# How the softmax sums of two attentions reach the rows of their heads: eight products, or one product and a broadcast by DMA

## The reference

```
# sparse attention (dsa): the keys outside a query's top 128 are masked
logits = (q . k) * scale - slope[head] * |q_pos - k_pos|    # masked where not selected
p = softmax(logits);  out = p @ v
# latent attention (mla): q and k of 64 + 32 features from latent projections
logits = (q . k) * scale                                    # masked after the query's chunk of 64
p = softmax(logits);  out = p @ v
```

## Time and profile before

| | |
|---|---|
| median of 3 runs | 2496.99 us (2496.9 to 2497.02) |
| the profiled execution: time, span | 2499.49 us, 2497.7 us |
| mean granted TensorE clock | 0.997 |
| busy: TensorE, weight load, VectorE, ScalarE, GpSimd | 99%, 79%, 54%, 40%, 44% |
| sparse attention, latent attention | about 1456 to 1502 us, 2025 to 2071 us |

### The profile page before, as it was taken

The page is one execution under the profiler, slowest core; times in us unless marked ns, Lnnn a source line. Parts: engine busy times, 40 slices in busy tenths (PEclk is TensorE's granted clock), DMA queues, the critical chain, the costliest instruction groups (busy, mean ns, idle before and its releaser), DMA issues.

```text
span 2497.7 us, 31897 instructions
## 1 busy us (share of the span) xinstructions
PE 2460.7 (99%) x11826; PEld 1975.9 (79%) x11826; DVE 1351.0 (54%) x2136; ACT 988.2 (40%) x1386; POOL 1102.8 (44%) x560
## 2 busy tenths in 40 slices
PE   9999999999999999999999999999999999999998
PEld 6658888887777788888877878888888758888887
DVE  7856635634666465365338655551554465652553
ACT  6553222235555432223334254532344243532333
POOL 7844444444332344444443413544444313544443
PEclk9999999999999999999999999999999999999999
DMA  7535546533322365564353312324333122324322
GB/s 205 151 91 171 186 142 202 164 89 110 98 68 72 88 208 165 164 195 135 90 146 85 102 34 77 94 76 117 93 87 91 64 68 68 85 80 114 100 76 70
DMA packets 403610, 282.09 MB, mean 113 GB/s; under 512 B 10867, under 2 KB 382707, under 8 KB 403484
## 3 DMA queue, kind: packets, MB, share of 16 engines
q1 hardware_dynamic: 389660, 230.09, 32.6%
q10 hardware_dynamic: 13824, 50.34, 5.4%
HBM read 269.73 MB, written 2.12 MB: 109 GB/s over the span
## 4 chain that ended last, share of the span: by engine, by line
PE 92%; DVE 3%; ACT 3%; issue 1%; POOL 1%; DMA 0%; SPq 0%; DVEq 0%; ACTq 0%
PE ps L762 27%; PE ps L763 27%; PE ps L764 27%; PE ps L1387 1%; PE ps L1583 1%; PE ps L1149 1%; PE ps L1123 1%; PE ps L1262 1%; PE ps L1237 1%; PE ps L1111 1%; PE ps L1108 1%; DVE u_lo L1746 1%; PE ps L1525 0%; ACT weight_hi L2728 0%; PE ps L1251 0%
## 5 line engine op out<-in xcount | busy, mean ns | idle before, releaser
L2582 POOL TENSOR_TENSOR weight_lo<-weight_raw,weight_hi 128x1024 fp32r<-128x1024 f32 (+3 forms) x416 | 940.4, 2282 | 1316.2 <-ACT weight_hi L2728 1193.5
L764 PE MATMUL ps<-u_hi,weight_lo 128*128 128x512 f32 (+1 forms) x2424 | 916.1, 378 | 0.0
L762 PE MATMUL ps<-u_hi,weight_hi 128*128 128x512 f32 (+1 forms) x2216 | 866.1, 391 | 8.1 <-POOL weight_lo L2582 2.0
L763 PE MATMUL ps<-u_lo,weight_hi 128*128 128x512 f32 (+1 forms) x2216 | 855.8, 386 | 0.0
L2728 ACT ACTIVATE weight_hi<-weight_raw 128x2048 fp32r<-128x2048 f32 (+2 forms) x213 | 363.2, 1705 | 576.0 <-PE ps L764 544.1
L764 PEld LDWEIGHTS ps<-u_hi,weight_lo 128*128 128x128 f32 x2424 | 455.8, 188 | 85.6
L762 PEld LDWEIGHTS ps<-u_hi,weight_hi 128*128 128x128 f32 x2216 | 416.1, 188 | 114.2 <-issue 15.8
L763 PEld LDWEIGHTS ps<-u_lo,weight_hi 128*128 128x128 f32 x2216 | 416.3, 188 | 84.7 <-issue 2.9
L764 PE MATMUL ps<-act_hi,weight_lo 128*128 128x512 f32 (+1 forms) x748 | 281.5, 376 | 0.0
L762 PE MATMUL ps<-act_hi,weight_hi 128*128 128x512 f32 (+1 forms) x704 | 269.5, 383 | 0.0
L763 PE MATMUL ps<-act_lo,weight_hi 128*128 128x512 f32 (+1 forms) x704 | 269.2, 382 | 0.0
(11 more groups left out here) (347 smaller groups left out, 2753.2 us busy)
## 6 DMA issues: line engine op xcount, KB each, us to landing
weight_raw<-in_ffn_w_up SPq DMA_DIRECT2D x132, 512.0 KB, 5.2
arena<-in_ada_w ACTq DMA_DIRECT2D x96, 512.0 KB, 5.7
weight_raw<-in_ffn_w_down SPq DMA_DIRECT2D x64, 704.0 KB, 4.7
weight_raw<-in_ffn_w_gate SPq DMA_DIRECT2D x44, 512.0 KB, 4.0
weight_raw<-in_ev_w_in SPq DMA_DIRECT2D x10, 1024.0 KB, 6.2
weight_raw<-in_conv_w_pw SPq DMA_DIRECT2D x16, 512.0 KB, 6.3
weight_raw<-in_ple_w_gate SPq DMA_DIRECT2D x16, 512.0 KB, 3.8
weight_raw<-in_attn_w_qkv SPq DMA_DIRECT2D x16, 512.0 KB, 5.4
```

The source lines that it names most:

```text
L762: pe.matmul(bank, w[0], x[0], start=start, stop=False)
L763: pe.matmul(bank, w[0], x[1], start=False, stop=False)
L764: return pe.matmul(bank, w[1], x[0], start=False, stop=stop)
L2582: low_part = pool.tensor_tensor(w_lo[r][:, cols], raw[r][:, cols], w_hi(k0 + j)[:, cols].bitcast(F32), ALU.subtract)
```

## The change

In the spreads with a = 0, 2 and 4 of both attentions, TensorE makes one product instead of eight: `rowinv`, 8 columns wide, is the stationary operand and the identity the moving one, so that 8 rows of 128 come out (head, then block). ScalarE copies the 8 rows to SBUF (`inverse_rows`), waits for that copy, and stores them to a table in device memory (`inverse_kept`) on its own queue. In the next odd step, after its three first exponentials, it waits for the store and issues a second transfer that reads each head's 4 rows as one row of 512 and repeats it on the head's 64 partitions of `sq[0]`. VectorE's multiply waits for that transfer instead of ScalarE's copy. The last spread of each attention (a = 6) stays as it was.

```diff
+        inverse_kept = nc.dram_tensor("inverse_kept", [6, 2 * NB, P], F32).ap()
...
+        inverse_rows = tmp[0:2 * NB, S:S + P]
...
+        spread_stored, spread_landed = sem("spread_stored"), sem("spread_landed")
...
                     if a > 0:
                         pe.wait_ge(spread_copied, p0 + a // 2)
+                    if a < G - 2:
+                        pe.matmul(ps[0:2 * NB, 3, 0:P], rowinv[:, 0:2 * NB], ident, start=True, stop=True).then_inc(sums_spread, 1)
+                        return
                     for b in range(NB):
...
-                        dve.wait_ge(spread_copied, n.next(spread_copied))
+                        copied = n.next(spread_copied)
+                        if g < G + 1:
+                            dve.wait_ge(spread_landed, n.next(spread_landed, 16))
+                        else:
+                            dve.wait_ge(spread_copied, copied)
                         dve.tensor_tensor(act_tmp[(g - 3) // 2 % 2], ps[:, 2], sq[0], ALU.mult).then_inc(o_copied, 1)
...
                         for b in range(NB - 1):
                             exponential(g, b)
+                        if g % 2 == 1 and g >= 3:
+                            kept = inverse_kept[3 * (kind == "mla") + g // 2 - 1]
+                            sc.wait_ge(spread_stored, n.next(spread_stored, 16))
+                            sc.dma_start(sq[0], bass.AP(kept.tensor, kept.offset, [[S, 2], [0, 64], [1, S]])).then_inc(spread_landed, 16)
...
                         if g >= 4:
                             sc.wait_ge(o_copied, o1 + g // 2 - 1)
-                        sc.activation(sq[0], ps[:, 3], ACT.Copy).then_inc(spread_copied, 1)
+                        if g < G:
+                            kept = inverse_kept[3 * (kind == "mla") + g // 2 - 1]
+                            sc.activation(inverse_rows, ps[0:2 * NB, 3, 0:P], ACT.Copy).then_inc(spread_copied, 1)
+                            sc.wait_ge(spread_copied, n.next(spread_copied))
+                            sc.dma_start(kept, inverse_rows).then_inc(spread_stored, 16)
+                        else:
+                            sc.activation(sq[0], ps[:, 3], ACT.Copy).then_inc(spread_copied, 1)
+                            n.take(spread_copied, 1)
```

## The result

The changed kernel takes 2510.14 us (median of 6 runs, 2508.0 to 2511.63) against 2496.94 for the kernel before (6 runs, 2496.55 to 2498.75): 13.2 us or 0.5% slower, ratio 1.0051, interval 1.0041 to 1.0062. The forecast was slower, 2519 in a range of 2506 to 2546.

A forecast was written before the change was run, and what follows sets the result against it. TensorE, busy 99% of the span, was taken to bound the kernel before; late broadcasts would cost 19.0 us with TensorE's gain inside, plus 3 for the clock: +22 us on 2496.99, so 2519.0, range 2506 to 2546.

The forecast's parts named there:

- What bounds the pairs: VectorE's multiply in odd steps would wait 3 to 5 us in six places for a broadcast shared by 2 engines.
- L: Time from the broadcast's issue to its landing: taken as 7.6 us, with 5.8 us of data; otherwise 7.0 to 11.5.
- L - 4.4: Net loss of each of six pairs, TensorE's gain inside: 7.6 - 4.43 us each, 19.0 us in all.
- The issue time: On ScalarE's queue: issues take 0.34 us, and the broadcast goes out when the odd step's three exponentials are done.
- The sum at its lowest: Six pairs' loss with the broadcast landing in 7.0 us and nothing added for the clock: 15 us.
- the case of 16 engines: Rival: 16 engines share the broadcast, it lands in 3.0 to 3.4 us, time 2493.8 us; chance 0.11.
- TensorE's gain: Six shorter spreads save 3.4 us in all, as ScalarE's copy holds the third transpose behind each.
- The rival that nothing is freed: Rival: one product drains the array as eight do, so the 3.4 us are missing: 2522 us; no separate chance given.
- the full 4.8: TensorE's work saved over six spreads, 0.80 us each, of which not all was expected to get through.
- The clock: After TensorE's idle gaps of 3 to 5 us the granted clock falls, costing 3 us over six pairs (0 to 9).
- What was hidden: The store, landing in about 1.7 us, and the second issue of 0.34 us on ScalarE's queue would be hidden.

The follow-up runs named there:

- two halves: The changed kernel with its one broadcast issued as two transfers, one per head: 2494.71 us, ratio 0.9988 to the kernel before.
- four engines: The changed kernel with the broadcast's source pattern given an outermost count of 4 (same bytes, wrong rows): 2495.18 us, 1.9 below the kernel before.
- the product alone: The changed kernel with both transfers left out, VectorE multiplying by what the buffer still holds: 2494.52 us, ratio 0.9987 to the kernel before.
- the unwaited broadcast: The changed kernel with both transfers made, but the broadcast sent to an unread buffer and VectorE's multiply not waiting for it: 2494.60 us.
- the count of 16: The changed kernel with the broadcast's source pattern given an outermost count of 16 (same bytes, wrong rows): 2493.97 us, 3.6 below the kernel before.
- the count of 8: The changed kernel with the broadcast's source pattern given an outermost count of 8 (same bytes, wrong rows): 2494.89 us, 2.2 below the kernel before.
- the eight products made again: The changed kernel with the eight products made before the one in each of the six spreads: 2514.87 us, ratio 1.0071 to the kernel before.
- the second trace of the change: The changed kernel as it is, timed again beside the later kernels on the same chip: 2510.14 us (5 runs), ratio 1.0060 to the kernel before.

## Why the prediction was right, and where its sizes were off

*What bounds the pairs.* Right. All six multiplies wait for the broadcast, which is shared by 2 engines as the small packets of the earlier trace rows had suggested; four outermost counts gave four engine counts, and with 16 or 8 engines or two halves the loss is gone. The rule of the Trainium skill that the prediction quoted (DMA: Bandwidth & Descriptors, "Why a DMA increments its semaphore by 16 and not by 1") agrees with these traces for two sides with different counts as well: 2 and 128 gave 2, 4 and 128 gave 4, 8 and 128 gave 8.

*The landing.* L = 7.6 was taken, 7.1 measured. The issue takes longer than supposed (0.52 us instead of 0.34) and with 16 engines the landing is 3.5 rather than 3.0, but the data go faster than was taken: 25.4 GB/s an engine, the best bulk figure of the earlier trace rows and not the middle of the two, which is 5.2 us for 128 KB instead of 5.8. (1.8 us of start, 0.2 more of issue and 5.2 are 7.2, against 7.1.) 0.5 us in six pairs is 3 us too much.

The Trainium skill gives about 27 GiB/s, which is 29 GB/s, as the bandwidth of an engine (DMA: Bandwidth & Descriptors, "Specifications"). The 25.4 GB/s seen here are 12% below it. With that figure, as an estimate (131 KB by 29 are 4.5 us, and 1.8 us of start: 6.3 - 4.4 in six pairs, and 3), the sum would have come out at 2511, near the measured time, but with a landing of 6.3 us where 7.1 was measured: the issue time, next, makes up for it.

*The issue time*: this term of the sum was mis-sized most. The broadcast was reckoned from the end of the three exponentials; it goes out 1.46 and 1.13 us ahead of that in the two first pairs and 0.7 in the others, since ScalarE's queue runs ahead of its engine. Counted from the attention's first scores, the issue was put at 1468.9 - 1456.33 = 12.6 and came at 1464.43 - 1453.16 = 11.3; the multiply was put at 20.2 and came at 19.0, which is 2.3 us late against 3.5. Over the six pairs the issues come 5.3 us early in all. L - 4.4 a pair should have read about L - 5.3: at 7.1 us 1.8 a pair, 11 in all, and 11.3 were measured in the trace. For the same reason the change would break even at a landing near 5.3 us, not 4.4: four engines, at 5.0 to 5.3 us, still left a gain of 1.9.

Both errors point the same way. Corrected for them the forecast of +22 reads about +14, against 13.2 measured. The sum at its lowest (L = 7.0 and nothing for the clock) gave +15, still more than was measured. The range held because its lower end, 2506, was set to leave out the case of 16 engines, and not by how far these two terms might be off: in that there is luck, and the measured time lies 4 us above it.

*TensorE's gain.* 3.4 was worked out; 2.9 to 3.6 below before were measured for the two halves, the product alone, the unwaited broadcast and the count of 16, and 2.2 for the count of 8, and the traces of the product alone and of the count of 16 show 3.0. The pair of instructions was put at 0.22 us and holds TensorE for 0.32, so that the third pairs have 0.7 to gain instead of 0.8: the sum should have read 3.2. ScalarE's copy holds the third transpose, as said: it waits 0.24 us for L3020 in the first pair. The rival that nothing is freed falls by the interval, and the full 4.8 by the traces.

*The clock.* 3 us was taken (0 to 9), about 3 measured, and it is the part that varies: the change's slowest run is 7 us above its fastest. In the trace of the change it fell only after the longer gaps: after 3.16 and 2.75 us at the second spread of the two attentions, and not after the 1.00 to 1.68 us of the later ones. No rule comes out of the other traces: with the eight products made again it fell after 2.05 and 2.29 us too, and in the second trace of the change it did not after 2.77.

*What was hidden.* The issues and the traffic: right, 0.1 us by the kernel in which nobody waits. The store was hidden behind the exponentials only because the broadcast was reckoned from their end. Since the broadcast is issued ahead of it, the store has less time: in four pairs of the change it had landed within 1.5 to 2.75 us, when the third exponential started. In the two first pairs it may have been what the broadcast waited for, which is not shown, and in one pair of the two halves it was, with 3.34 us.

## What to carry to other kernels

The shape of a transfer can cost more than its bytes: here the outermost count of the source decided how many engines carried 256 KB (2, 4, 8 or 16), and a broadcast written as two rows repeated 64 times fell to two. Count the small packets in a quiet window of the trace, one for each engine, and split such a transfer or put the large count outermost. A work saving of 0.5 us a pair on the busiest engine is worth making only if the replacement's latency fits the time up to its consumer; measure that time from when the queue can issue, not from when the engine is done.

## What the runs showed of the hardware that was not expected

- ScalarE's queue issued a transfer while up to three exponentials ahead of it had yet to end, up to 1.46 us before the last of them did; in four pairs of six it went out 0.01 us after the last of them had started. A transfer that must follow an engine's result needs a wait of its own (the store here has one).
- A store of 8 rows of 512 B took 3.34 us to land in one pair (two halves), where in others the transfer that waits for it was issued 1.2 to 1.8 us after it.
- Two DMA engines by themselves moved 25.4 GB/s each, no more than the 20.6 to 25 that one of 16 reached in bulk loads.
- Idle stretches of TensorE of 2 to 4.4 us brought the granted clock to parts at the 1.2 GHz level (0.64 to 0.87 in windows of 4 us at and behind a gap of about 3 us; 0.50, which is that level throughout, over 4 us behind a gap of 4.4) in some places of a run and not in others. The same program spread over 7 us from run to run, where the kernel before spread over 0.6 us on the same chip (over 2.6 and 3.6 us, with more runs, on two others).
- The issue of the broadcast took 0.52 us (0.60 with an outermost count of 8) and of the 8-row store 0.27, where plain loads take 0.34.
